# Early sums for the fifth down product, and the running sum's start copied on chip

## The chip, the cores and the metric

The kernel runs on one core of a Trainium2 chip. Its time is the device time in microseconds, the median of several executions. Everything is float32: each matmul operand is split into a high and a low part of type fp32r, and a product is three matmuls (high x high, high x low, low x high).

## The reference, cut to what matters

```python
def conv_ffn(x, norm_g, w_up, conv_w, conv_b, w_down):
    h = rms_norm(x, norm_g)
    a, b = jnp.split(h @ w_up, 2, axis=-1)
    a = causal_depthwise_conv(a, conv_w) + conv_b      # width 3
    return (jax.nn.silu(a) * b) @ w_down

def reference(x, ...):
    for l in range(2):                                 # DEPTH
        x = x + hybrid_mixer(x, ...)                   # attention and retention
        x = x + conv_ffn(x, ...)
    return rms_norm(x, final_norm)
```

The input is 512 tokens by 1024; w_down is 2816 by 1024. The change touches only the last product of each layer, `g @ w_down`.

## The kernel before, in words

**The down projection.** `g` (2816 x 512 tokens) and `w_down` are cut into 2 x 2 quarters and multiplied with 7 quarter products instead of 8 (the scheme of Strassen and Winograd). The weights' quarters are W11, W21, W12 and W22; four products take a single quarter or W12 + W22, and three take a running sum that grows in place from W11: W11 + W12, then + W22, then + W21. Each quarter comes in 6 pieces (`PIECES`), five of 128 x 1024 numbers (524288 bytes) and a last one of half that. So there are 7 x 6 = 42 *units* (`UNITS_DOWN`), and unit u is piece u % 6 of product u // 6:

- k = 0: W11; k = 1: W11 + W12; k = 2: + W22; k = 3: W21; k = 4, the fifth: W12 + W22; k = 5: W22; k = 6: the full running sum.
- The raw weights of k = 0, 3, 4 and 5 are loaded into *raw slots*: 4 in `w_raw` (numbers 0 to 3) and 4 in `far_raw` (4 to 7, `FAR` on). The low part of a unit takes the place of its raw data. For k = 1, 2 and 6 the raw data is in `t_raw`, six tiles for the running sum, and the raw slot holds only the low part.
- The high part of a unit goes into one of 8 *high slots* (`w_hi`, `far_hi`), in turn.
- `RAW_ORDER`, `RAW_SLOT`, `HI_ORDER` and `HI_SLOT` (lines 63 to 68) are these plans, written out by hand.

**Who does what.** Each engine has its own list of work and goes through it in order; a wait holds up all that stands behind it.

- SyncE (`load_down`, line 575) issues the plain loads. The 6 pieces of the running sum's W11 (`load_sum`, line 571) and those of units 1 to 3 alternate while the last up product runs. Then each further unit is loaded when its raw slot is free, that is when TensorE is done with the slot's earlier unit (semaphore `s_unit`), in the order in which slots come free: units 18, 19, 24, 25, 20, 21, 22, 23, 26, 27, 28 and so on. Units 26 and 27 take the slots of units 18 and 19. After them come the first four slabs of the next layer.
- GpSimd issues the accumulating transfers, which add a piece from memory onto a tile: `first_sums` (line 700) adds W12 onto the running sum, `gated` multiplies the last pair of g, `further_sums` (line 706) adds W22 and then W21 onto the running sum, each piece when VectorE has made the low part that used the sum before it (`s_qlo`), and then adds W22 onto the raw data of the fifth product's units 24 to 29, each when W21's sum of the same piece (`s_tsum[j]`) and the unit's load (`s_fetch`) have landed.
- ScalarE makes the high parts (`unit_high`, line 864) and those of `g`'s chunks (`chunk_high`, line 879), four units ahead of TensorE. Among the first units stand `last_quarter`, `tap` and `silu` of the last pair.
- VectorE makes the low parts (`unit_low`, line 1412; `chunk_low`, line 1421) three units ahead, the sums of chunks, and takes the products out of PSUM.
- TensorE (`down_unit` in layer 0, `token_unit` in layer 1) runs a unit as 24 matmuls of 256 columns in layer 0 and 12 of 512 in layer 1, after the waits for `s_qlo` and, at even units, `s_clo` (the chunk's low part). A chunk of g serves two units. All matmuls come out of the helper `three_open`, lines 1768 to 1770.

The lines of the profile that matter below: L569 the load of a unit, L573 that of the running sum, L697 an accumulating transfer onto the running sum, L717 one onto a unit of the fifth product, L727 GpSimd's product of the last pair, L877 a unit's high part, L891 and L893 a chunk's, L854 the last quarter of the up products, L862 and L1400 the convolution, L1418 a unit's low part, L1427 and L1429 a chunk's.

Of the kernel before, what the change touches and what calls it, by code (L numbers as in the profile page):

```python
# [61 lines left out]
FAR = RING  # L62
RAW_ORDER = [3, 1, 0, 2, FAR, FAR + 1, FAR + 2, FAR + 3, 3, 1, FAR + 2, FAR + 3, 3, 1, FAR + 2, FAR + 3, 3, 1,
             0, 2, FAR + 2, FAR + 3, 3, 1, FAR, FAR + 1, 0, 2, FAR + 2, FAR + 3, 3, 1, FAR, FAR + 1, 0, 2,
             FAR, FAR + 1, FAR + 2, FAR + 3]
RAW_SLOT = [RAW_ORDER + [FAR, FAR + 1], RAW_ORDER + [3, 1]]
HI_ORDER = [(2, 1, 0, FAR, FAR + 1, FAR + 2, FAR + 3, 3)[u % 8] for u in range(UNITS_DOWN)]
HI_SLOT = [HI_ORDER[:39] + [FAR, FAR + 1, 3], HI_ORDER]
HI_AFTER = (0, 1, 2, 3, 4, 5, 6, 7)
# [3 lines left out]
def before(slots, u):  # L73

    return max((v for v in range(u) if slots[v] == slots[u]), default=None)

# [78 lines left out]
def trunk(nc, xt, wts, wdn, par, consts, rope, decay, last, out):  # L155
    with ExitStack() as ctx:
# [32 lines left out]
        far_hi = sb("far_hi", [P, 4, SLAB], F32R, u_lo_at)  # L189
        w_hi_at = at[0]  # L190
# [213 lines left out]
        s_tland = [sem(f"s_tland{j}") for j in range(2)]  # L404
# [6 lines left out]
        s_unit = sem("s_unit")  # L411
        s_gain = sem("s_gain")
# [54 lines left out]
        def slot_raw(s):  # L467

            return w_raw[:, s, :] if s < RING else far_raw[:, s - RING, :]

        def slot_lo(s):

            return w_lo[:, s, :] if s < RING else far_lo[:, s - RING, :]
# [44 lines left out]
        def _(sp):  # L518
# [46 lines left out]
            def load_unit(l, u):  # L565
# [3 lines left out]
                sp.dma_start(unit_raw(l, u), wdn[l * 4 + quarter, :, j * 1024:j * 1024 + piece(j)]).then_inc(s_fetch[RAW_SLOT[l][u]], 16)  # L569

            def load_sum(l, j):

                sp.dma_start(t_raw[:, j, 0:piece(j)], wdn[l * 4 + W11, :, j * 1024:j * 1024 + piece(j)]).then_inc(s_tland[int(j > 1)], 16)  # L573

            def load_down(l):
# [3 lines left out]
                for k in range(3):  # L579
                    sp.wait_ge(s_prod, done + k + 1)  # L580
                    load_sum(l, 2 * k)
                    load_sum(l, 2 * k + 1)
# [5 lines left out]
                for u in sorted(LOADED[PIECES:], key=lambda u: before(RAW_SLOT[l], u)):  # L588
                    sp.wait_ge(s_unit, l * UNITS_DOWN + before(RAW_SLOT[l], u) + 1)
                    load_unit(l, u)  # L590
# [61 lines left out]
        def _(pool):  # L652
# [47 lines left out]
            def first_sums(l):  # L700

                for j in range(PIECES):
                    pool.wait_ge(s_tland[int(j > 1)], l * (32 + 32 * (j > 1)) + 32 + 32 * (j > 1))
                    add_piece(l, j, W12)
# [1535 lines left out]
```

## Time and profile before

| | us |
|---|---|
| median of 3 runs | 1579.28 |
| lowest and highest | 1578.63, 1582.32 |
| the profiled execution | 1583.04 |
| its span in the profile | 1581.2 |
| TensorE busy | 1563.6 |
| VectorE busy | 1163.5 |
| ScalarE busy | 768.9 |
| GpSimd busy | 250.8 |

The times of the rows below are counted from the start of the profiled execution's span; what the span leaves out of its time is 1.8 us. The down projection runs from 674 to 789 us in layer 0 and from 1458 to 1575 us in layer 1. In the page's rows a group ends with its idle time and what ended it; in a timeline the bracket says how long the engine stood idle and who released it.

### The profile page before, as it was taken

To read this page: it belongs to the slowest core of one execution; us is meant where nothing else is said; L and a number is where in the kernel's file an instruction comes from. 1 tells how busy PE (TensorE), PEld (TensorE's weight loads), DVE (VectorE), ACT (ScalarE), POOL (GpSimd) and SP (SyncE) were. 2 spreads that over 40 slices of the span, in tenths; PEclk is the share of its full clock that TensorE was granted. 3 is DMA by queue.
4 is the path that set the end of the run, shared out by engine and by line. 5 is a ranking of instruction groups with operands and counts; after the bars stand their busy time and mean duration, and the time that the engine had idled before them with its cause. 6 is when DMAs were issued, how large, how long until landed. Compare 5 with 4: busy or idle time off the path is not lost.

```text
span 1581.2 us, 22764 instructions
## 1 busy us (share of the span) xinstructions
PE 1563.6 (99%) x9106; PEld 1379.8 (87%) x9106; DVE 1163.5 (74%) x1295; ACT 768.9 (49%) x982; POOL 250.8 (16%) x270
## 2 busy tenths in 40 slices
PE   9999999999999999999999999999999999999988
PEld 7888888888888999999988888888888899999866
DVE  7257876786679787796972678667766897777967
ACT  5344334542355555663533533355422565556636
POOL 4000000000230222331240000000002212223400
PEclk9999999999999999999999999999999999999999
DMA  5342222222227888999133422222223388888991
GB/s 195 97 122 78 78 81 93 80 68 93 93 94 239 240 240 241 280 224 275 67 104 97 120 78 76 75 92 80 68 93 101 103 248 235 238 241 275 231 267 53
DMA packets 66628, 231.41 MB, mean 146 GB/s; under 512 B 7392, under 2 KB 7904, under 8 KB 66528
## 3 DMA queue, kind: packets, MB, share of 16 engines
q1 hardware_dynamic: 52272, 182.93, 33.7%
q0 software_dynamic: 12096, 41.95, 14.6%
q10 hardware_dynamic: 2160, 5.12, 1.2%
q8 instruction: 72, 1.18, 0.3%
q14 instruction: 28, 0.23, 0.0%
HBM read 225.78 MB, written 2.10 MB: 144 GB/s over the span
## 4 chain that ended last, share of the span: by engine, by line
PE 91%; DMA 4%; issue 2%; DVE 1%; POOL 1%; ACT 0%; DVEq 0%; POOLq 0%
PE ps L1762 18%; PE ps L1764 18%; PE ps L1763 18%; PE ps L1768 10%; PE ps L1770 10%; PE ps L1769 10%; DMA far_raw<-wdn 2%; PE ps L1891 1%; DMA w_raw<-wdn 1%; PE ps L1880 1%; PE ps L1858 1%; PE ps L1862 1%; DMA w_raw<-wts 1%; DMA far_raw<-wts 1%; POOL g_raw L727 1%
## 5 line engine op out<-in xcount | busy, mean ns | idle before, releaser
L1762 PE MATMUL ps<-u_hi,w_hi 128*128 128x512 f32 x768 | 301.3, 392 | 0.0
L1763 PE MATMUL ps<-u_lo,w_hi 128*128 128x512 f32 x768 | 299.3, 390 | 0.0
L1764 PE MATMUL ps<-u_hi,w_lo 128*128 128x512 f32 x768 | 299.1, 389 | 0.0
L1200 DVE TENSOR_TENSOR w_lo<-w_raw,w_hi 128x1024 fp32r<-128x1024 f32 x158 | 208.5, 1332 | 68.3 <-ACT w_hi L766 68.1
L766 ACT ACTIVATE w_hi<-w_raw 128x1024 fp32r<-128x1024 f32 x158 | 164.1, 1052 | 77.3 <-DMA w_raw<-wts 70.9
L1764 PEld LDWEIGHTS ps<-u_hi,w_lo 128*128 128x128 f32 x768 | 144.2, 188 | 30.4
L1762 PEld LDWEIGHTS ps<-u_hi,w_hi 128*128 128x128 f32 x768 | 144.4, 188 | 28.4
L1763 PEld LDWEIGHTS ps<-u_lo,w_hi 128*128 128x128 f32 x768 | 144.4, 188 | 28.3
L1768 PE MATMUL ps<-comb_hi,far_hi 128*128 128x256 f32 x576 | 161.1, 280 | 0.6 <-DVE far_lo L1363 0.2
L1769 PE MATMUL ps<-comb_lo,far_hi 128*128 128x256 f32 x576 | 160.8, 279 | 0.0
L1770 PE MATMUL ps<-comb_hi,far_lo 128*128 128x256 f32 x512 | 142.9, 279 | 0.0
L1768 PE MATMUL ps<-comb_hi,w_hi 128*128 128x256 f32 x432 | 121.6, 282 | 0.6 <-DVE cb L1385 0.3
L1769 PE MATMUL ps<-comb_lo,w_hi 128*128 128x256 f32 x432 | 120.7, 279 | 0.0
L1770 PE MATMUL ps<-comb_hi,w_lo 128*128 128x256 f32 x432 | 120.6, 279 | 0.0
L1768 PEld LDWEIGHTS ps<-comb_hi,far_hi 128*128 128x128 f32 x576 | 108.1, 188 | 1.5 <-issue 1.1
L1769 PEld LDWEIGHTS ps<-comb_lo,far_hi 128*128 128x128 f32 x576 | 108.1, 188 | 0.0
L727 POOL TENSOR_TENSOR g_raw<-cc,cb 128x512 f32<-128x512 f32 x36 | 73.6, 2063 | 185.5 <-ACT cc L848 185.5
L1770 PEld LDWEIGHTS ps<-comb_hi,far_lo 128*128 128x128 f32 x512 | 96.1, 188 | 0.0
L1363 DVE TENSOR_TENSOR far_lo<-far_raw,far_hi 128x1024 fp32r<-128x1024 f32 x48 | 58.6, 1222 | 42.3 <-ACT far_hi L835 42.3
L1768 PEld LDWEIGHTS ps<-comb_hi,w_hi 128*128 128x128 f32 x432 | 81.0, 188 | 2.3 <-DVE cb L1385 1.3
L1769 PEld LDWEIGHTS ps<-comb_lo,w_hi 128*128 128x128 f32 x432 | 81.1, 188 | 0.0
L1770 PEld LDWEIGHTS ps<-comb_hi,w_lo 128*128 128x128 f32 x432 | 81.1, 188 | 0.0
(307 smaller groups left out, 3715.8 us busy)
## 6 DMA issues: line engine op xcount, KB each, us to landing
w_raw<-wts SPq DMA_DIRECT2D x212, 512.0 KB, 3.5
far_raw<-wts SPq DMA_DIRECT2D x56, 512.0 KB, 4.2
t_raw<-wdn POOLq DMA_DIRECT2D x30, 512.0 KB, 9.8
w_raw<-wdn SPq DMA_DIRECT2D x24, 512.0 KB, 7.6
w_raw<-wts POOLq DMA_DIRECT2D x18, 512.0 KB, 10.5
far_raw<-wts POOLq DMA_DIRECT2D x16, 512.0 KB, 7.2
far_raw<-wdn SPq DMA_DIRECT2D x16, 512.0 KB, 8.7
t_raw<-wdn SPq DMA_DIRECT2D x10, 512.0 KB, 5.7
```

What stands on the lines that cost most here:

```text
L727: nc.gpsimd.tensor_tensor(g_raw[:, f, :], cc[:, h, :], cb[:, h, :], ALU.mult).then_inc(s_gf, 1)
L766: nc.scalar.activation(w_hi[:, s, :], w_raw[:, s, :], ACT.Copy).then_inc(s_hi, 1)
L1200: nc.vector.tensor_tensor(w_lo[:, s, :], w_raw[:, s, :], w_hi[:, s, :].bitcast(F32), ALU.subtract).then_inc(s_lo, 1)
L1363: nc.vector.tensor_tensor(part_lo(l, n, k), part_raw(l, n, k), part_hi(l, k).bitcast(F32), ALU.subtract).then_inc(s_elo, 1)
L1762: nc.tensor.matmul(dst, a_hi, b_hi, start=start, stop=False)
L1763: nc.tensor.matmul(dst, a_hi, b_lo, start=False, stop=False)
L1764: return nc.tensor.matmul(dst, a_lo, b_hi, start=False, stop=stop)
L1768: nc.tensor.matmul(dst, a_hi, b_hi, start=start, stop=False, skip_group_check=True)
L1769: nc.tensor.matmul(dst, a_hi, b_lo, start=False, stop=False, skip_group_check=True)
L1770: return nc.tensor.matmul(dst, a_lo, b_hi, start=False, stop=stop, skip_group_check=True)
L1858: nc.tensor.matmul(psf[:, E0 + BLK[c]:E0 + BLK[c] + WIDTH[c]], q2[:, h, t * P:(t + 1) * P], k2[:, h, 0:WIDTH[c]], start=(c != 3), stop=Fal ...
L1862: mm = nc.tensor.matmul(psf[:, E0 + BLK[c]:E0 + BLK[c] + WIDTH[c]], q_lo[p][:, h % 2, t * P:(t + 1) * P], k2[:, h, 0:WIDTH[c]], start=Fals ...
```

## The change

- Two *spare* raw slots, 8 and 9 (`SPARE`), lie in the place of the high slots 6 and 7. These two serve as high slots once each, for units 5 and 6; from unit 8 on the high parts go round 6 slots instead of 8. Units 26 and 27 are loaded into the spare slots when units 5 and 6 are done (`vacated`), and the slots of the later units move with them. Units 36 to 41 use the two as well, for their low parts.
- The sums W12 + W22 of the fifth product's first four pieces (`EARLY_SUMS`) are issued between the W22 and the W21 sums of the running sum; those of units 28 and 29 stay behind the W21 sums.
- The running sum's W11 is no longer loaded: ScalarE copies each of units 0 to 5 from its raw slot into `t_raw`, just ahead of making its high part. `first_sums` waits for the copy.

```diff
--- before.py
+++ after.py
@@ -60,12 +60,14 @@
 UNITS_DOWN = 7 * PIECES
 CHUNKS = 21
 FAR = RING
+SPARE = FAR + 4
 RAW_ORDER = [3, 1, 0, 2, FAR, FAR + 1, FAR + 2, FAR + 3, 3, 1, FAR + 2, FAR + 3, 3, 1, FAR + 2, FAR + 3, 3, 1,
-             0, 2, FAR + 2, FAR + 3, 3, 1, FAR, FAR + 1, 0, 2, FAR + 2, FAR + 3, 3, 1, FAR, FAR + 1, 0, 2,
-             FAR, FAR + 1, FAR + 2, FAR + 3]
-RAW_SLOT = [RAW_ORDER + [FAR, FAR + 1], RAW_ORDER + [3, 1]]
-HI_ORDER = [(2, 1, 0, FAR, FAR + 1, FAR + 2, FAR + 3, 3)[u % 8] for u in range(UNITS_DOWN)]
+             0, 2, FAR + 2, FAR + 3, 3, 1, FAR, FAR + 1, SPARE, SPARE + 1, 0, 2, FAR + 2, FAR + 3, 3, 1, FAR, FAR + 1,
+             SPARE, SPARE + 1, FAR + 2, FAR + 3, FAR, FAR + 1]
+RAW_SLOT = [RAW_ORDER, RAW_ORDER]
+HI_ORDER = [(2, 1, 0, FAR, FAR + 1, FAR + 2, FAR + 3, 3)[u] if u < 8 else (FAR + 1, 3, 2, 1, 0, FAR)[u % 6] for u in range(UNITS_DOWN)]
 HI_SLOT = [HI_ORDER[:39] + [FAR, FAR + 1, 3], HI_ORDER]
+EARLY_SUMS = 4
 HI_AFTER = (0, 1, 2, 3, 4, 5, 6, 7)
 SUM_K = (1, 2, 4, 5)
 
@@ -73,6 +75,13 @@
 def before(slots, u):
 
     return max((v for v in range(u) if slots[v] == slots[u]), default=None)
+
+
+def vacated(l, u):
+
+    if RAW_SLOT[l][u] >= SPARE and before(RAW_SLOT[l], u) is None:
+        return HI_SLOT[l].index(RAW_SLOT[l][u] - 2)
+    return before(RAW_SLOT[l], u)
 
 
 LOADED = [u for u in range(UNITS_DOWN) if u // PIECES in (0, 3, 4, 5)]
@@ -187,6 +196,9 @@
         u_lo_at = at[0]
         u_lo = sb("u_lo", [P, KT, S], F32R)
         far_hi = sb("far_hi", [P, 4, SLAB], F32R, u_lo_at)
+        spare_at = u_lo_at + 2 * 4 * SLAB
+        spare_raw = sb("spare_raw", [P, 2, SLAB], F32, spare_at)
+        spare_lo = sb("spare_lo", [P, 2, SLAB], F32R, spare_at)
         w_hi_at = at[0]
         w_hi = sb("w_hi", [P, RING, SLAB], F32R)
         w_odd = sb("w_odd", [P, RING, SLAB], F32, w_hi_at)
@@ -401,7 +413,7 @@
         s_c11 = sem("s_c11")
         s_c21 = sem("s_c21")
         s_c22 = sem("s_c22")
-        s_tland = [sem(f"s_tland{j}") for j in range(2)]
+        s_tcopy = sem("s_tcopy")
         s_tsum = [sem(f"s_tsum{j}") for j in range(PIECES)]
         s_qhi = sem("s_qhi")
         s_qlo = sem("s_qlo")
@@ -409,6 +421,7 @@
         s_clo = sem("s_clo")
         s_csum = sem("s_csum")
         s_unit = sem("s_unit")
+        s_spare = sem("s_spare")
         s_gain = sem("s_gain")
         s_tok = sem("s_tok")
         s_moved = sem("s_moved")
@@ -466,11 +479,11 @@
 
         def slot_raw(s):
 
-            return w_raw[:, s, :] if s < RING else far_raw[:, s - RING, :]
+            return w_raw[:, s, :] if s < RING else far_raw[:, s - RING, :] if s < SPARE else spare_raw[:, s - SPARE, :]
 
         def slot_lo(s):
 
-            return w_lo[:, s, :] if s < RING else far_lo[:, s - RING, :]
+            return w_lo[:, s, :] if s < RING else far_lo[:, s - RING, :] if s < SPARE else spare_lo[:, s - SPARE, :]
 
         def slot_hi(s):
 
@@ -566,11 +579,8 @@
 
                 k, j = divmod(u, PIECES)
                 quarter = {0: W11, 3: W21, 4: W12, 5: W22}[k]
-                sp.dma_start(unit_raw(l, u), wdn[l * 4 + quarter, :, j * 1024:j * 1024 + piece(j)]).then_inc(s_fetch[RAW_SLOT[l][u]], 16)
-
-            def load_sum(l, j):
-
-                sp.dma_start(t_raw[:, j, 0:piece(j)], wdn[l * 4 + W11, :, j * 1024:j * 1024 + piece(j)]).then_inc(s_tland[int(j > 1)], 16)
+                landed = s_fetch[RAW_SLOT[l][u]] if RAW_SLOT[l][u] < SPARE else s_spare
+                sp.dma_start(unit_raw(l, u), wdn[l * 4 + quarter, :, j * 1024:j * 1024 + piece(j)]).then_inc(landed, 16)
 
             def load_down(l):
 
@@ -578,15 +588,13 @@
                 load_unit(l, 0)
                 for k in range(3):
                     sp.wait_ge(s_prod, done + k + 1)
-                    load_sum(l, 2 * k)
-                    load_sum(l, 2 * k + 1)
                     load_unit(l, k + 1)
                 sp.wait_ge(s_prod, done + 4)
                 load_unit(l, 4)
                 sp.wait_ge(s_prod, done + 5)
                 load_unit(l, 5)
-                for u in sorted(LOADED[PIECES:], key=lambda u: before(RAW_SLOT[l], u)):
-                    sp.wait_ge(s_unit, l * UNITS_DOWN + before(RAW_SLOT[l], u) + 1)
+                for u in sorted(LOADED[PIECES:], key=lambda u: vacated(l, u)):
+                    sp.wait_ge(s_unit, l * UNITS_DOWN + vacated(l, u) + 1)
                     load_unit(l, u)
                 for i in range(RING if l + 1 < DEPTH else 0):
                     sp.wait_ge(s_unit, l * UNITS_DOWN + max(u for u in range(UNITS_DOWN) if RAW_SLOT[l][u] == i) + 1)
@@ -700,22 +708,35 @@
             def first_sums(l):
 
                 for j in range(PIECES):
-                    pool.wait_ge(s_tland[int(j > 1)], l * (32 + 32 * (j > 1)) + 32 + 32 * (j > 1))
+                    pool.wait_ge(s_tcopy, l * PIECES + j + 1)
                     add_piece(l, j, W12)
 
+            def add_fifth(l, j):
+
+                u = 4 * PIECES + j
+                if RAW_SLOT[l][u] >= SPARE:
+                    pool.wait_ge(s_spare, 32 * (l + 1))
+                else:
+                    pool.wait_ge(s_fetch[RAW_SLOT[l][u]], 16 * (1 + l * arrivals_of_layer(u) + arrivals(u)))
+                nc.gpsimd.dma_start(unit_raw(l, u), wdn[l * 4 + W22, :, j * 1024:j * 1024 + piece(j)],
+                                    accum_op=ALU.add).then_inc(s_tsum[j], 16)
+
             def further_sums(l):
 
-                for k, quarter in ((1, W22), (2, W21)):
-                    for j in range(PIECES):
-                        pool.wait_ge(s_qlo, l * UNITS_DOWN + k * PIECES + j + 1)
-                        add_piece(l, j, quarter)
                 for j in range(PIECES):
-                    u = 4 * PIECES + j
-                    s = RAW_SLOT[l][u]
+                    pool.wait_ge(s_qlo, l * UNITS_DOWN + PIECES + j + 1)
+                    add_piece(l, j, W22)
+                for j in range(EARLY_SUMS):
+                    pool.wait_ge(s_tsum[j], l * 64 + 32)
+                    add_fifth(l, j)
+                for j in range(PIECES):
+                    pool.wait_ge(s_qlo, l * UNITS_DOWN + 2 * PIECES + j + 1)
+                    if j < EARLY_SUMS:
+                        pool.wait_ge(s_tsum[j], l * 64 + 48)
+                    add_piece(l, j, W21)
+                for j in range(EARLY_SUMS, PIECES):
                     pool.wait_ge(s_tsum[j], l * 64 + 48)
-                    pool.wait_ge(s_fetch[s], 16 * (1 + l * arrivals_of_layer(u) + arrivals(u)))
-                    nc.gpsimd.dma_start(unit_raw(l, u), wdn[l * 4 + W22, :, j * 1024:j * 1024 + piece(j)],
-                                        accum_op=ALU.add).then_inc(s_tsum[j], 16)
+                    add_fifth(l, j)
 
             def gated(l, n):
 
@@ -864,16 +885,19 @@
             def unit_high(l, u):
 
                 k, j = divmod(u, PIECES)
-                if k in (1, 2, 6):
-                    act.wait_ge(s_tsum[j], l * 64 + {1: 16, 2: 32, 6: 48}[k])
-                elif k == 4:
-                    act.wait_ge(s_tsum[j], l * 64 + 64)
+                if k in (1, 2):
+                    act.wait_ge(s_tsum[j], l * 64 + 16 * k)
+                elif k in (4, 6):
+                    act.wait_ge(s_tsum[j], l * 64 + (48 if (k == 4) == (j < EARLY_SUMS) else 64))
                 else:
                     act.wait_ge(s_fetch[RAW_SLOT[l][u]], 16 * (1 + l * arrivals_of_layer(u) + arrivals(u)))
                 if before(HI_SLOT[l], u) is None:
                     act.wait_ge(s_prod, 7 * (l * SPLIT + SPLIT - 1) + HI_AFTER[u])
                 else:
                     act.wait_ge(s_unit, l * UNITS_DOWN + before(HI_SLOT[l], u) + 1)
+                if k == 0:
+                    act.wait_ge(s_prod, 7 * (l * SPLIT + SPLIT - 1) + j // 2 + 1)
+                    nc.scalar.activation(t_raw[:, j, 0:piece(j)], unit_raw(l, u), ACT.Copy).then_inc(s_tcopy, 1)
                 nc.scalar.activation(slot_hi(HI_SLOT[l][u])[:, 0:piece(j)], unit_raw(l, u), ACT.Copy).then_inc(s_qhi, 1)
 
             def chunk_high(l, c):
```

## Rows read from the trace of the kernel before

**Rows 1.** The page: busy time, share of the span, instructions, by engine.

```profile
PE 1563.6 (99%) x9106; PEld 1379.8 (87%) x9106; DVE 1163.5 (74%) x1295; ACT 768.9 (49%) x982; POOL 250.8 (16%) x270
```

**Rows 2.** Waits of TensorE, whole run: us in total, times, longest.

```profile
PE ps L1768 <- DVE chunk_lo L1429: 6.5, 6, 1.8
```

**Rows 3.** TensorE's timeline: start us, us, instruction, [idle before <- releaser].

```profile
685.39 0.28 PE L1768 MATMUL ps<-chunk_hi,far_hi 128*128 128x256 f32 x1
...
752.07 0.42 PE L1768 MATMUL ps<-chunk_hi,far_hi 128*128 128x256 f32 x1 [1.78 <-DVE chunk_lo L1429]
...
1470.76 0.48 PE L1768 MATMUL ps<-far_hi,chunk_hi 128*128 128x512 f32 x1
...
1518.85 0.47 PE L1768 MATMUL ps<-far_hi,chunk_hi 128*128 128x512 f32 x1 [0.51 <-DVE chunk_lo L1429]
...
1529.60 0.47 PE L1768 MATMUL ps<-w_hi,chunk_hi 128*128 128x512 f32 x1 [0.96 <-DVE chunk_lo L1429]
...
1534.59 0.50 PE L1768 MATMUL ps<-far_hi,chunk_hi 128*128 128x512 f32 x1 [2.02 <-DVE w_lo L1418]
...
1539.43 0.47 PE L1768 MATMUL ps<-far_hi,chunk_hi 128*128 128x512 f32 x1 [1.82 <-DVE chunk_lo L1429]
...
1541.45 0.63 PE L1769 MATMUL ps<-far_lo,chunk_hi 128*128 128x512 f32 x1
```

**Rows 4.** Stretches: length, busy by engine, PEclk, DMA share, GB/s.

```profile
665.00:670.00 5.00, 5.00 (x44) 5.00 (x43) 3.53 (x5) 5.00 (x7) 5.00 (x4) 1.00 1.03 414
1485.00:1490.00 5.00, 5.00 (x26) 4.15 (x24) 4.79 (x6) 3.79 (x5) 1.71 (x2) 1.00 1.07 211
1540.00:1545.00 5.00, 5.00 (x17) 3.94 (x16) 5.00 (x6) 3.20 (x4) 0.00 (x0) 0.66 0.00 1
```

**Rows 5.** The chain that ended last, layer 1: start us, us, step.

```profile
1510.22 9.57 DMA w_raw<-wdn
...
1522.86 13.21 DMA far_raw<-wdn
1536.09 1.07 ACT far_hi L877
```

**Rows 6.** GpSimd's timeline, layer 0 and layer 1.

```profile
699.13 0.87 POOL L697 DMA_DIRECT2D t_raw<-wdn  x1 [0.60 <-DVE far_lo L1418]
...
1485.34 0.86 POOL L697 DMA_DIRECT2D t_raw<-wdn  x1 [0.61 <-DVE far_lo L1418]
...
1520.32 0.86 POOL L717 DMA_DIRECT2D w_raw<-wdn  x1 [18.04 <-DMA w_raw<-wdn]
```

**Rows 7.** Landing of the sums issued at 1485, 1498, 1500, 1520 (four), 736.

```profile
DMA to landing us min/median/max: 9.8/9.8/9.8
...
DMA to landing us min/median/max: 11.0/11.6/12.2
...
DMA to landing us min/median/max: 15.3/16.7/18.1
...
DMA to landing us min/median/max: 5.7/11.9/15.2
...
DMA to landing us min/median/max: 12.6/13.5/14.5
```

**Rows 8.** ScalarE's timeline, layer 0 and layer 1.

```profile
666.18 1.05 ACT L891 ACTIVATE chunk_hi<-g_raw 128x1024 fp32r<-128x1024 f32 x1
...
674.14 0.60 ACT L854 ACTIVATE ca<-ps 128x512 f32<-128x512 f32 x1
...
1450.69 1.05 ACT L891 ACTIVATE chunk_hi<-g_raw 128x1024 fp32r<-128x1024 f32 x1
...
1461.26 0.58 ACT L854 ACTIVATE ca<-ps 128x512 f32<-128x512 f32 x1
```

**Rows 9.** VectorE's timeline, layer 0.

```profile
677.15 0.74 DVE L1400 SCALAR_TENSOR_TENSOR cc<-ca,pars,cc 128x512 f32<-128x512 f32 x1
...
682.32 2.06 DVE L1427 SCALAR_TENSOR_TENSOR chunk_lo<-g_raw,chunk_hi 128x768 fp32r<-128x768 f32 x1
```

## The prediction

> **What bounds the kernel now.** I read the page first: TensorE is busy 99% of a span of 1581.2 us [rows 1]. So a change that takes nothing away from TensorE can win only where TensorE stands still. The second view, its waits, puts almost all of that on one line, the matmul of the split products, which waits for VectorE's low parts [rows 2]. The third, TensorE's timeline, says where. I call the pieces of the down projection's weights units, 0 to 41, in the order of use (unit = 6 x product + piece), and count products from 0; the fifth product is k = 4, units 24 to 29. A full unit takes 2.72 us in layer 1 (12 matmuls, 0.227 us apart). In layer 1 the restarts at 1518.85, 1529.60, 1534.59 and 1539.43 are the first matmuls of units 22, 26, 27 and 28 [rows 3]: three of the four are of the fifth product. The matmuls between them are left out there, a full unit being 12 of them. From start to start the intervals before them are 0.7, 1.1, 2.3 and 2.1 us above 2.72, and units 22, 28 and 29 themselves take 0.1, 1.4 and 0.3 too long; in sum **8.0 us**. The 1.4 is the clock: from 1541 us on matmuls start 0.43 us apart, and the stretch 1540 to 1545 shows a granted clock of 0.66 after the three idle spells [rows 3, 4]: some of its time at 1.2 GHz instead of 2.4. In layer 0 the same four restarts (at 733.21, 744.06, 747.22 and 752.07; the last stands in [rows 3], and all are in the sum of [rows 2]) give 0.8, 1.0, 0.4 and 2.1, and 1.6 goes to the clock: **5.9 us**. All that this change can win is so 13.9 us, 0.9%.
>
> Why they are late: the chain of waits goes from TensorE at 1510 to the reload of a raw slot (9.6 us), to GpSimd's accumulating transfer for unit 28 (13.2 us), to ScalarE's high part, to VectorE's low parts, to the matmul at 1539.43 [rows 3, 5]. GpSimd's timeline shows the hole: after the sums of units 24 and 25, issued at 1500, it waits 18.0 us, until 1520.32, for unit 26's raw data [rows 6], whose slot comes free only with unit 18. But the last views say that the transfers were hardly idle meanwhile: a stretch with sums alone moves 211 GB/s, one with mostly plain loads 414 [rows 4], so a sum of 524288 bytes takes 2.5 us of the engines and a load 1.27. The sums issued at 1498.2 and 1499.6 land after 11.0 and 12.2 us, those of units 24 and 25 after 15.3 and 18.1 [rows 7]: at 1509.2, 1511.8, 1515.5 and 1518.8. That is 3.84 us for each full sum where loads run beside them (9.6 us for 2.5 sums, piece 5 being half a piece).
>
> **The change part by part.**
>
> 1. *The running sum's W11 from the chip.* Removed: 6 loads a layer on SP's queue (5.5 full ones, 7 us of transfer time), just ahead of the units' loads. On the rule: the Trainium skill, page "DMA: Bandwidth & Descriptors", section on bandwidth, puts loads from HBM at about 358 GB/s; by it the loads cost 8.1 us instead of 7; the row shows 414 and decides, and the sum below would stay. Added: 6 copies on ScalarE ahead of units 0 to 5's high parts. Two such operations back to back start 0.95 us apart, so 5.3 us a layer. Behind them on ScalarE are the last quarter, the taps and SiLU of the last pair. From the chunk copy at 666.18 there are now 12 operations to the last quarter, 11.4 us: it starts at about 677.6 in layer 0 instead of 674.14 [rows 8], and VectorE's convolutions, which started at 677.15, start when the first tap is done, at 679.1 [rows 9]. VectorE runs without a gap there (the chunk's low part, 2.06 us from 682.32, ended at 684.4) [rows 9], and TensorE takes that chunk at 685.39 [rows 3]. It is now ready at 686.4: **a new stall of 1.1 us at unit 4 of layer 0**. In layer 1 ScalarE had stood waiting for landings, which now come earlier: counted from the same chunk copy, 1450.69 + 11.4 is 1462.1, 0.8 us behind the 1461.26 of before [rows 8]; the stall is 0.3 (unit 4 starts at 1470.76 [rows 3], with 0.7 us to spare, and VectorE comes 1.0 later). The first W22 sum is issued 2 us (layer 0) and 1 us (layer 1) later. The copies' waits for s_prod cost nothing: ScalarE has waited for the fourth part product before (chunk 0).
>
> 2. *Units 26 and 27 in the spare tiles.* Their loads move from after units 18 and 19 to after units 5 and 6, at about 1476 and 1479 on SP's queue, ahead of those of units 20 on. That adds 2.5 us of transfers where the W22 sums run; the W11 loads had left some 3 us of backlog there, which goes. The high parts' ring shrinks from 8 to 6. ScalarE makes them at most some 4 units ahead, so the shorter ring adds no wait.
>
> 3. *The order of the sums.* Before: 6 W22, 6 W21, units 24, 25 | hole | 26, 27, 28, 29. After: 6 W22, units 24 to 27, 6 W21, units 28, 29. Units 26 and 27 are so in time by over 15 us: their stalls go, 2.3 + 1.1 in layer 1 and 1.4 in layer 0. Each of W21's first four waits for the early sum of the same piece, with three more sums in the queue behind it, so the queue doesn't run dry. But **unit 28's sum now stands behind everything**, and waits until W21's fourth piece (counted from 0) has landed.
>
> *When it lands, layer 1.* W22's last sum landed at 1485.34 + 9.8 = 1495.1 [rows 6, 7]; now 0.5 later (1 us of start, 2.5 of loads, less 3 of backlog). Four sums at 2.5 us, as unit 20's load is issued at 1500.7 only: 1505.6. Five W21 sums at 3.84: 1524.8. Then unit 28's own, behind half a sum. Nearest rows: of the four sums issued from 1520.32 on, the first, with nothing ahead, took 5.7 us [rows 7], the third, unit 28's, with two ahead, 13.2 [rows 5], and by the median of 11.9 between second and third the second, with one ahead, 10.6 [rows 7]. I take 8.1, the middle of 5.7 and 10.6: 1532.9. From landing to matmul it took 1539.43 - 1536.1 = 3.3 us, so TensorE starts unit 28 at 1536.2 instead of 1539.43: **3.2 us gained**. Without the stalls of units 26 to 28 TensorE would be there at 1534.2 (1539.43 - 1.1 - 2.3 - 2.1, and the 0.3), so 2.0 us of waiting are left. Bounds: 5.7 us at the least gains 2 us more, which ends the wait; 13.2 us costs 5.1, a loss of 1.9.
>
> *Layer 0.* W22's last sum, issued at 699.13, also took 9.8 us and landed at 708.9 [rows 6]; now 2.1 + 2.5 - 3 = 1.6 later, 710.5. Unit 20's load goes out at 714.1, so only three sums run at 2.5 us: 718.0. Six at 3.84: 741.0. Plus 8.1 and 3.3: 752.4, against 752.07 [rows 3] (before, the sum was issued at 736.2 and landed after 12.6 us, at 748.8 [rows 7]). **Nothing gained (-0.3)**; the stall at unit 4 is swallowed, since the sums, not TensorE, set that time.
>
> 4. *What stays.* Unit 22's stall (0.7 and 0.8 us) is a plain load that goes out when TensorE leaves unit 16 and takes as long as the 9.6 us one of the chain [rows 5]; its slot and the company it has stay. The clock fell after idle spells of which the last, 1.8 us in both layers, are like what is left; I let it fall again. The next layer's first slabs are loaded earlier; TensorE doesn't wait for them before either.
>
> Sum: -3.2 + 0.3 = 2.9 us less. The profiled execution took 1583.0 us (span 1581.2, 1.8 around it), 3.8 above the median of the three runs, whose spread is 3.7; I take the 2.9 from the median 1579.28 and get **1576.5 us**.
>
> **The rivals.** *No stall at unit 28.* If the sums keep 2.5 us beside the loads, nine sums after 1495.6 end at 1518, unit 28's lands by 1526 and TensorE never waits: 8.0 - 0.8 = 7.2 us in layer 1, 5.9 - 0.8 = 5.1 in layer 0, less 1.4 of new stalls: 10.9 us, 1568.4. For it: the rate of sums alone. Against: the four landings from 1509 to 1519. 0.17.
> *The stall stays and the clock doesn't fall*, being one spell and not three: 1.5 us more in each layer, 1573.5. Against: layer 0 fell after only 0.8, 0.3 and 1.8 us. 0.13.
> *Slower*: unit 28 is the price. It decides once its sum lands after 1536.1 (748.8 in layer 0), which is so if the sum takes over 11.3 us beside the loads of units 30 to 33, as the one of 13.2 did. At 13.2 both layers lose 5.1 more: 1576.5 + 10.2 = 1586.7 at the worst, half of it 1581.6; past 1584 it is slower. 0.13.
> *Nothing moves*: the sums end when they did, since their number is the same and only their order differs, 1579 +/- 1. For it: layer 0 above. 0.12.
>
> **How the numbers follow.** My forecast, stalls moved to unit 28 and 3 us won, gets 0.45. About 0.3%, 4.7 us, is what a measurement of this kernel can tell from no change: 1574.5 and 1584.0 are the bounds. Faster: the first two rivals, 0.17 + 0.13 = 0.30. Same: 0.45 + 0.12 = 0.57. Slower: 0.13. The range reaches down to the case with no stall, 1568, and up past the middle of the slower case to 1585.
>
> **What would show it.** Right: no idle time before units 26 and 27 in either layer; one wait of 1 to 3 us at unit 28 that ends with the accumulating transfer into w_raw (its slot is now 0); W21 sums issued from about 1498 on with gaps of 2.5 us, not at the low parts' pace; GpSimd's 18.0 us wait gone and one of some 15 us before unit 28's sum; 12 copies into t_raw on ScalarE and no t_raw loads on SP's queue; a new wait of about 1 us at unit 4 of layer 0; a clock under 0.8 after unit 28. Wrong: no wait at unit 28, or one of over 5 us; idle TensorE in units 6 to 21 (a high part held back by the ring of 6, or W22's sums late by the two loads).

## The result, and the profile after

The changed kernel takes 1587.27 us, the median of 8 executions (1583.36 to 1588.42). The kernel before, run beside it, takes 1579.38 (8 executions, 1574.94 to 1582.32). The ratio is 1.0041, with a 95% interval from 1.0030 to 1.0053: **slower by 6.5 us** by the ratio (7.9 by the two medians), more than the 4.7 us that the prediction takes as what can be told from no change. It is the case that the prediction calls "slower", and lies above the range.

| | before [rows 1] | after |
|---|---|---|
| profiled execution | 1583.04 | 1587.19 |
| TensorE idle for VectorE's chunk parts | 6.5 us, 6 times, longest 1.8 [rows 2] | 13.7 us, 7 times, longest 5.1 |
| ScalarE busy, instructions | 768.9, 982 | 779.3, 994 |

The page of the kernel after: busy time by engine.

```profile
PE 1562.8 (99%) x9106; PEld 1379.5 (87%) x9106; DVE 1163.5 (73%) x1295; ACT 779.3 (49%) x994; POOL 250.7 (16%) x270
```

TensorE's waits, whole run (us in total, times, longest); it answers to [rows 2].

```profile
PE ps L1792 <- DVE chunk_lo L1453: 13.7, 7, 5.1
```

TensorE's timeline of the kernel after (start us, us, instruction, idle before it and releaser); it answers to [rows 3].

```profile
692.32 0.36 PE L1792 MATMUL ps<-chunk_hi,far_hi 128*128 128x256 f32 x1 [0.76 <-DVE chunk_lo L1453]
...
735.59 0.36 PE L1792 MATMUL ps<-chunk_hi,w_hi 128*128 128x256 f32 x1 [1.75 <-DVE chunk_lo L1453]
...
756.96 0.55 PE L1792 MATMUL ps<-chunk_hi,w_hi 128*128 128x256 f32 x1 [5.13 <-DVE chunk_lo L1453]
...
1523.56 0.47 PE L1792 MATMUL ps<-w_hi,chunk_hi 128*128 128x512 f32 x1 [1.11 <-DVE chunk_lo L1453]
...
1528.46 0.47 PE L1792 MATMUL ps<-far_hi,chunk_hi 128*128 128x512 f32 x1 [0.54 <-DVE chunk_lo L1453]
...
1543.57 0.47 PE L1792 MATMUL ps<-w_hi,chunk_hi 128*128 128x512 f32 x1 [3.97 <-DVE chunk_lo L1453]
```

These are the first matmuls of units 6, 22 and 28 in layer 0, and of units 22, 24 and 28 in layer 1 (unit 24 of layer 0 waited 0.47 us and is not shown). No restart stands at units 26 and 27 any more, in either layer. One stands at unit 28, of 5.1 and 4.0 us; none of those of before was over 2.02 [rows 3].

GpSimd's timeline of the kernel after, layer 1; it answers to [rows 6].

```profile
1490.78 2.09 POOL L721 DMA_DIRECT2D far_raw<-wdn  x2
1497.46 1.74 POOL L721 DMA_DIRECT2D spare_raw<-wdn  x2 [4.58 <-DMA spare_raw<-wdn]
1504.67 0.86 POOL L705 DMA_DIRECT2D t_raw<-wdn  x1 [5.47 <-DMA far_raw<-wdn]
1513.76 2.63 POOL L705 DMA_DIRECT2D t_raw<-wdn  x3 [2.95 <-DMA spare_raw<-wdn]
1531.35 0.86 POOL L721 DMA_DIRECT2D w_raw<-wdn  x1 [14.96 <-DMA t_raw<-wdn]
```

The sums of units 24 to 27 are out by 1499 and the hole of 18.0 us is gone. In its place GpSimd waits 15.0 us, until W21's piece 4 has landed, before it may issue unit 28's sum.

The landing of the sums in the kernel after, from issue: the last W22 sum (1490.25), the three W21 sums of 1514, unit 28's sum (1531.35); then the plain loads issued from 1510 to 1518. It answers to [rows 7].

```profile
DMA to landing us min/median/max: 11.4/11.4/11.4
...
DMA to landing us min/median/max: 13.9/16.8/18.8
...
DMA to landing us min/median/max: 8.9/8.9/8.9
...
DMA to landing us min/median/max: 10.0/12.5/13.4
```

The chain that ended last, layer 1 (start us, us, step); it answers to [rows 5].

```profile
1514.32 13.19 DMA w_raw<-wdn
1527.55 3.79 issue
1531.35 8.87 DMA w_raw<-wdn
1540.24 1.06 ACT w_hi L901
1541.33 1.22 DVE w_lo L1442
1542.56 0.88 DVE chunk_lo L1453
1543.57 0.47 PE ps L1792
```

The first step is unit 28's plain load. The 3.79 us called "issue" is no work of GpSimd: its timeline above puts that wait down to the transfer into t_raw, W21's piece 4, issued at 1514.3 and landed 16.8 us later, at 1531.1. The sum itself then takes 8.87 us, and 3.3 us lie from its landing to the matmul, as before.

### The profile page after: what moved, and what is told of

It is laid out like the page before. It is cut to its first block, busy times and chain, and to the rows that moved or that the text cites. A ratio compares the mean times of both kernels' runs of the same rounds, so it can differ in the third digit from the quotient of the medians.

```text
span 1585.4 us, 22772 instructions
## 1 busy us (share of the span) xinstructions
PE 1562.8 (99%) x9106; PEld 1379.5 (87%) x9106; DVE 1163.5 (73%) x1295; ACT 779.3 (49%) x994; POOL 250.7 (16%) x270
## 4 chain that ended last, share of the span: by engine, by line
PE 51%; DMA 3%; DVE 2%; issue 1%; ACT 1%; DVEq 0%; POOLq 0%
PE ps L1786 9%; PE ps L1788 9%; PE ps L1787 9%; PE ps L1792 7%; PE ps L1794 7%; PE ps L1793 7%; DMA w_raw<-wdn 3%; PE ps L1915 1%; PE ps L1904 1%; DMA w_raw<-wts 0%; PE ps L1882 0%; PE ps L1886 0%; DVE far_lo L1442 0%; PE ps L2039 0%; PE ps L1926 0%
## 5 line engine op out<-in xcount | busy, mean ns | idle before, releaser
L1793 PEld LDWEIGHTS ps<-comb_lo,w_hi 128*128 128x128 f32 x432 | 81.1, 188 | 0.0
## 6 DMA issues: line engine op xcount, KB each, us to landing
t_raw<-wdn POOLq DMA_DIRECT2D x30, 512.0 KB, 11.6
w_raw<-wts POOLq DMA_DIRECT2D x18, 512.0 KB, 10.1
```

The source lines that it names most:

```text
L1793: nc.tensor.matmul(dst, a_hi, b_lo, start=False, stop=False, skip_group_check=True)
```

## The experiments

A measure that serves all of them, worked out from the starts of units in TensorE's timeline: the time from the start of unit 0 to that of unit 28, and to that of unit 36, in each layer. It leaves out what the rest of the kernel adds. Each row is one profiled execution. In layer 0 the matmuls of 256 columns run at one of several paces, which no edit chose (see the last section). In "another order alone", at 113.3 ns a matmul, unit 28 comes after 72.1 us, 1.1 of them waiting; in "six early sums, W11 loaded", at 120.0 ns, after 74.9 with no wait. So a difference of up to 4 us in layer 0 between rows with short waits or none need be no effect of an edit.

| kernel | median us | to unit 28, layer 0 / 1 | to unit 36, both layers |
|---|---|---|---|
| before, the profile of the rows | 1579.38 | 78.1 / 81.0 | 201.1 |
| before, profiled again | | 78.2 / 78.2 | 195.8 |
| after | 1587.27 | 81.2 / 81.0 | 203.5 |
| after, profiled again | 1586.01 | 80.9 / 81.1 | 204.6 |
| early sums, W11 loaded | 1585.24 | 79.5 / 81.6 | 204.2 |
| copies alone | 1581.83 | 80.9 / 80.3 | 200.1 |
| no early sums | 1579.86 | 79.4 / 78.2 | 196.2 |
| six early sums | 1568.27 | 74.1 / 74.7 | 187.4 |
| six early sums, W11 loaded | 1567.63 | 74.9 / 74.7 | 188.8 |
| another order alone | 1571.06 | 72.1 / 76.2 | 187.7 |
| six early sums, the last pair's product earlier | 1570.58 | 74.1 / 74.7 | 187.4 |

**1. The early sums alone.** The changed kernel, but W11 is loaded onto the running sum as before.

```diff
+                    load_sum(l, 2 * k)
+                    load_sum(l, 2 * k + 1)
                     load_unit(l, k + 1)
...
-                    pool.wait_ge(s_tcopy, l * PIECES + j + 1)
+                    pool.wait_ge(s_tland[int(j > 1)], l * (32 + 32 * (j > 1)) + 32 + 32 * (j > 1))
...
-                    nc.scalar.activation(t_raw[:, j, 0:piece(j)], unit_raw(l, u), ACT.Copy).then_inc(s_tcopy, 1)
```

> The changed kernel with the running sum's W11 loaded from memory again, as before the change; the early sums and the spare slots stay. Theory A (the queue of sums sets unit 28): the copies only delayed the start of the W22 sums by 1.9 us in layer 0 and 0.8 us in layer 1, so unit 28's wait shrinks by about that, the 0.9 us stall at unit 6 of layer 0 goes, and the rest of the wait, 3 us or more in each layer, stays: 1 to 3 us faster than the changed kernel, still slower than or the same as before. Theory B (the on-chip copies are what costs): the loss of 6.5 us goes altogether, the time is that of before or better and unit 28's wait is under 1.5 us.

Measured: 1585.24 (12 executions), ratio 1.0034 [1.0021, 1.0047]. TensorE's waits, its first matmul of unit 28 in layer 0, and GpSimd's issue of unit 28's sum in layer 1:

```profile
PE ps L1795 <- DVE chunk_lo L1456: 10.6, 6, 3.4
...
755.16 0.55 PE L1795 MATMUL ps<-chunk_hi,w_hi 128*128 128x256 f32 x1 [3.44 <-DVE chunk_lo L1456]
...
1530.31 0.86 POOL L727 DMA_DIRECT2D w_raw<-wdn  x1 [14.96 <-DMA w_raw<-wdn]
```

The loss is there without the copies: by the ratios 5.4 of the 6.5 us come with the order and the tiles. The wait at unit 28 is 3.4 us in layer 0 and 3.1 in layer 1, as forecast, the one at unit 6 is gone, and GpSimd's wait of 15.0 us stands unchanged. In layer 1 unit 4 waited 1.1 us here, which was not forecast.

**2. The copies alone.** The kernel before, with W11 copied by ScalarE and not loaded; slots and order as before.

```diff
-                    load_sum(l, 2 * k)
-                    load_sum(l, 2 * k + 1)
...
+                if k == 0:
+                    act.wait_ge(s_prod, 7 * (l * SPLIT + SPLIT - 1) + j // 2 + 1)
+                    nc.scalar.activation(t_raw[:, j, 0:piece(j)], unit_raw(l, u), ACT.Copy).then_inc(s_tcopy, 1)
```

> The kernel before with only the W11 copies on ScalarE; ring, slots and order of sums of before. Theory A: stall of 1 us at unit 4 to 6 of layer 0, W22 sums start 2 us later there; units 26 to 28 wait as before (their stalls hang on the reload of unit 26's slot): within 2 us of before. Theory B: slower than before by 4 us or more.

Measured: 1581.83 (11 executions), ratio 1.0015 [1.0005, 1.0025], 2.4 us slower, a little more than the 2 us expected. TensorE's waits, the first matmul of unit 26 in layer 0, the stretch behind it (length, busy by engine, PEclk, DMA share, GB/s), and the landing of the last W22 sum in layer 1:

```profile
PE ps L1765 <- DVE chunk_lo L1426: 9.6, 6, 5.4
...
749.18 0.55 PE L1765 MATMUL ps<-chunk_hi,w_hi 128*128 128x256 f32 x1 [5.40 <-DVE chunk_lo L1426]
...
745.00:750.00 5.00, 0.82 (x4) 0.85 (x5) 2.36 (x2) 2.64 (x3) 0.00 (x0) 0.58 1.06 274
...
DMA to landing us min/median/max: 8.1/8.1/8.1
```

Without the W11 loads the last W22 sum lands after 8.1 us instead of 9.8 [rows 7]: the backlog that they left is worth 1.7 us, not 3. In layer 0 the wait at unit 26 grew from 0.8 us to 5.4, and the trace divides the 4.6 us. Counted from unit 0, unit 26's sum is issued 1.4 us later (61.1 against 59.7) and takes 8.8 us instead of 6.8, so it lands 3.4 us later; and TensorE comes 1.2 us earlier, at 113.3 ns a matmul instead of 118.7.

**3. All six sums early.** The changed kernel with one number changed.

```diff
-EARLY_SUMS = 4
+EARLY_SUMS = 6
```

> The changed kernel with EARLY_SUMS = 6: all six sums of the fifth product ahead of the W21 sums. Theory A: unit 28's sum no longer waits for W21's piece 4 but for its own load, which has the transfer engines more to itself, and lands at least 4 us earlier in each layer; unit 28 waits under 1 us, the clock stays at full speed, unit 22's stall shrinks; the W21 sums land by about 1550, ahead of unit 36: 10 us faster than the changed kernel, some 4 faster than before. Theory B: no faster than the changed kernel. A rival to A: the total work of the transfer engines is the bound, so the W21 sums are late for units 36 on and the wait reappears there, with the time of the changed kernel.

Measured: 1568.27 (5 executions), ratio 0.9922 [0.9905, 0.9939]: **some 12 us faster than before** (12.3 by the ratio, 11.1 by the medians), where some 4 were expected. TensorE's only wait of this kind (us in total, times, longest) and the matmul behind it, unit 6 of layer 0; GpSimd's timeline in layer 1, with the sums of units 28 and 29 and then five of W21's; and the landing of the loads issued from 1501 to 1509:

```profile
PE ps L1792 <- DVE chunk_lo L1453: 0.7, 1, 0.7
...
692.29 0.36 PE L1792 MATMUL ps<-chunk_hi,far_hi 128*128 128x256 f32 x1 [0.69 <-DVE chunk_lo L1453]
...
1509.68 0.86 POOL L721 DMA_DIRECT2D w_raw<-wdn  x1 [19.86 <-DMA w_raw<-wdn]
1511.50 0.86 POOL L721 DMA_DIRECT2D w_raw<-wdn  x1 [0.96 <-DMA w_raw<-wdn]
1512.04 4.74 POOL L705 DMA_DIRECT2D t_raw<-wdn  x5
...
DMA to landing us min/median/max: 2.8/4.1/5.3
```

GpSimd waits longer here than before, 19.9 us against 18.0 [rows 6], and it costs nothing, because what stands behind is not needed soon: W21's sums serve unit 36. All stalls of the fifth product are gone, unit 22's too. The loads land in 2.8 to 5.3 us, as no sums compete with them meanwhile.

**4. No early sum.** `EARLY_SUMS = 0` in the changed kernel: copies, spare tiles and the ring of 6 stay, the order is that of before.

> The changed kernel with EARLY_SUMS = 0: slots and early loads of units 26 and 27 and the copies stay, but the order of the sums is that of before, W21 ahead of the fifth product. Theory A: the queue has no hole and no sum waits for another's landing except unit 28's for its load (landed at 1527.5 in the changed kernel), so unit 28's sum lands 3 to 4 us earlier than in the changed kernel: its wait falls to 1 us or less, 6 to 9 us faster than the changed kernel. If instead unit 28's place behind all other sums is what costs (it stands behind the same number here), the wait stays at 4 to 5 us.

Measured: 1579.86 (12 executions), ratio 1.0004 [0.9992, 1.0016]. TensorE's first matmul of unit 26 in layer 0, then GpSimd's issue of unit 28's sum and TensorE's first matmul of unit 28 in layer 1:

```profile
747.63 0.36 PE L1792 MATMUL ps<-chunk_hi,w_hi 128*128 128x256 f32 x1 [1.17 <-DVE chunk_lo L1453]
...
1523.22 0.86 POOL L721 DMA_DIRECT2D w_raw<-wdn  x1 [12.47 <-DMA w_raw<-wdn]
...
1537.20 0.47 PE L1792 MATMUL ps<-w_hi,chunk_hi 128*128 128x512 f32 x1 [1.62 <-DVE chunk_lo L1453]
```

So tiles, ring and copies together cost nothing that shows, and bring nothing: unit 27 no longer waits, but unit 28 still does, 1.6 us in layer 1 and 1.5 in layer 0, and so does unit 26 (0.5 and 1.2). The expectation that unit 28's wait would fall to 1 us or less did not hold; the 7.4 us below the changed kernel's 1587.27 did. Against this run the changed kernel differs only in the order of the sums: its loss is the position of the four early sums and W21's, and with it unit 28's.

**5 and 6. Both kernels once more**, unedited, on another chip, to see how much of the first two profiles is theirs alone.

> The changed kernel once more, nothing edited. It asks how much of its 6.5 us is not in the down stage: in the profiles the down stages (start of unit 0 to start of unit 36, both layers) are 2.4 us longer than before, while the 256-column matmuls of layer 0's up stage start 118.7 ns apart in the changed kernel and 116.7 ns or less in the kernel before. If that pace is a matter of the single execution, it differs between two profiles of one kernel and the medians of many runs carry little of it; if it belongs to the kernel, this profile shows 118.7 ns again in layer 0 from 520 to 670 us, and the time is again 5 to 8 us above before.

> The kernel before once more, nothing edited. If the pace of the 256-column matmuls belongs to the execution, this profile shows another pattern than the first (113.3, 116.7 and 118.7 ns in other places) and unit 0 of layer 0 starts at another time than 673.9; if it belongs to the kernel, the pattern and the 673.9 come back. The stalls at units 22 and 26 to 28 should be there in either case, 5 to 8 us a layer with the slower clock behind them.

Measured: the changed kernel 1586.01 (10 executions), ratio 1.0034 [1.0020, 1.0048]; the profiled execution of the kernel before 1579.94, at its median of 1580.01. Counted from unit 0 of layer 1, the sums of the changed kernel land as in its first profile, unit 28's after 77.7 us in both. The stretches behind unit 28 (length, busy by engine, PEclk, DMA share, GB/s) of the kernel after, first profile:

```profile
755.00:760.00 5.00, 3.04 (x15) 3.07 (x16) 5.00 (x6) 3.41 (x5) 0.00 (x0) 0.66 0.04 9
1545.00:1550.00 5.00, 5.00 (x16) 3.92 (x16) 5.00 (x6) 3.07 (x4) 0.00 (x0) 0.67 0.00 0
```

And TensorE's waits and the same stretches in the second profile of the kernel before:

```profile
PE ps L1768 <- DVE chunk_lo L1429: 6.5, 6, 1.7
PE ps L1768 <- DVE w_lo L1418: 0.5, 1, 0.5
...
750.00:755.00 5.00, 3.25 (x28) 3.08 (x27) 4.32 (x5) 3.37 (x4) 0.00 (x0) 1.00 0.82 275
1540.00:1545.00 5.00, 5.00 (x22) 3.89 (x22) 5.00 (x5) 3.34 (x4) 0.00 (x0) 1.00 0.00 0
```

The clock stays at 1.00, where the profile of the rows had 0.66 [rows 4], and the wait of 2.02 us at unit 27 [rows 3] is one of 0.5. That first execution took 3.8 us more than the median, and these two things are in it: the kernel before has executions with them and without. How many have the fall, the mean granted clock of a whole execution suggests: it was 0.997 in the first profile and 0.999 in the second, and of 55 other executions of the kernel before, 17 had 0.998 or less. All 18 of the changed kernel had 0.995 to 0.998, and it has the fall in both profiles and both layers. Its second profile had 0.50 in the stretch 755 to 760.

**7. Six early sums, W11 loaded.** Edits 1 and 3 together.

> All six sums of the fifth product ahead of W21's, and W11 loaded from memory instead of copied: does the copy help once the order is right? Theory A: the 7 us of loads stand in the transfer queue ahead of the W22 sums, where there is slack once unit 28's sum is early; the 0.9 us stall at unit 6 of layer 0 goes: the time of the run with six early sums and copies (0.992 of before), within 2 us. If the copies matter, 3 us or more slower than that run.

Measured: 1567.63 (6 executions), ratio 0.9925 [0.9911, 0.9938], as with the copies (0.9922): they neither help nor cost once the order is right. The stall at unit 6 of layer 0 is gone with them, as in experiment 1.

**8. Another order alone.** The kernel before, with its slots, its ring and its loads; only the W21 sums are issued behind those of the fifth product.

```diff
-                for k, quarter in ((1, W22), (2, W21)):
-                    for j in range(PIECES):
-                        pool.wait_ge(s_qlo, l * UNITS_DOWN + k * PIECES + j + 1)
-                        add_piece(l, j, quarter)
+                for j in range(PIECES):
+                    pool.wait_ge(s_qlo, l * UNITS_DOWN + PIECES + j + 1)
+                    add_piece(l, j, W22)
...
+                for j in range(PIECES):
+                    pool.wait_ge(s_qlo, l * UNITS_DOWN + 2 * PIECES + j + 1)
+                    pool.wait_ge(s_tsum[j], l * 64 + 48)
+                    add_piece(l, j, W21)
```

> The kernel before with one edit: W21's sums are issued behind the fifth product's instead of ahead; slots, ring of 8 and loads of before. Theory A (what stands in the queue ahead of the fifth product's sums is what matters): GpSimd still waits for unit 26's load, freed by unit 18 at 1510, but the transfer engines are empty by then, so the load takes 4 us instead of 9.6, the sum lands by 1521 and unit 28's by 1529: all stalls from unit 22 on go, and the time is that of the run with six early sums, 9 to 12 us under before. Rival (the spare tiles are needed): units 26 to 28 still wait 2 us or more each layer, the gain is under 5 us.

Measured: 1571.06 (6 executions), ratio 0.9945 [0.9929, 0.9961]. GpSimd's timeline in layer 1 (sums of units 26 to 29, then four of W21's) and the landing of the loads issued from 1500 to 1509:

```profile
1508.60 0.86 POOL L716 DMA_DIRECT2D w_raw<-wdn  x1 [26.59 <-DMA w_raw<-wdn]
1511.28 0.86 POOL L716 DMA_DIRECT2D w_raw<-wdn  x1 [1.81 <-DMA w_raw<-wdn]
1517.41 0.86 POOL L716 DMA_DIRECT2D far_raw<-wdn  x1 [5.28 <-DMA far_raw<-wdn]
1520.52 0.86 POOL L716 DMA_DIRECT2D far_raw<-wdn  x1 [2.25 <-DMA far_raw<-wdn]
1521.06 3.86 POOL L697 DMA_DIRECT2D t_raw<-wdn  x4
...
DMA to landing us min/median/max: 3.5/3.6/3.8
```

An edit of the order brings some 9 of the 12 us with none of the change's parts. Unit 26's slot comes free as late as before, but its load takes some 3.6 us instead of 9.6 [rows 5], and nothing stands ahead of its sum. Not all stalls go, as had been expected: unit 28 still waits 1.1 us in layer 0 and 1.3 in layer 1, for a sum whose load goes out 57.2 us after unit 0; with the change's slots and the same order (experiment 3) it goes out after 51.8, and unit 28 does not wait.

**9. The last pair's product ahead of the last W12 sum.** The stall at unit 6 of layer 0 follows GpSimd's product of the last pair, so with six early sums it was issued one sum earlier.

```diff
-                first_sums(l)
+                first_sums(l, range(PIECES - 1))
                 gated(l, SPLIT - 1)
+                first_sums(l, (PIECES - 1,))
```

> All six early, with copies, and one more edit on GpSimd: the product of the last pair (L748) is issued ahead of the last W12 sum instead of behind it. In the changed kernel that last sum waits for ScalarE's sixth copy, and the product, which slows VectorE's operations beside it from 1.2 to 2.1 us, starts 1.8 us after it otherwise could. If that order makes the 0.9 us stall at unit 6 of layer 0, the stall shrinks to 0.3 us or less and the time is 0 to 1 us under the run with six early sums, which its timing can hardly tell; if the stall comes from ScalarE's copies alone, it stays at 0.9 us.

Measured: 1570.58 (6 executions), ratio 0.9933 [0.9916, 0.9951]: no gain. GpSimd's product, TensorE at unit 6, and ScalarE's SiLU:

```profile
683.40 4.23 POOL L748 TENSOR_TENSOR g_raw<-cc,cb 128x512 f32<-128x512 f32 x2 [4.26 <-ACT cc L870]
...
691.82 0.35 PE L1793 MATMUL ps<-chunk_hi,far_hi 128*128 128x256 f32 x1 [0.87 <-DVE chunk_lo L1454]
...
682.70 1.30 ACT L870 ACTIVATE cc<-cc 128x512 f32<-128x512 f32 x2
```

The product starts 0.5 us earlier than in experiment 3 (683.89), and what it waits for is ScalarE. The stall stays at 0.9 us, so GpSimd's queue is not its cause. ScalarE's copies are: without them (experiments 1 and 7) it is gone.

## Why the prediction was wrong, point by point

**Right.** The order's mechanism was told as it is. Units 26 and 27 are in time. "Unit 28's sum now stands behind everything" and waits for W21's piece 4, GpSimd for 15.0 us ("some 15"). The sum then takes 8.9 us (8.1 forecast) and 3.3 to the matmul (3.3). The ring of 6 adds no wait, the clock falls behind unit 28, and the W22 sums start 0.8 us later in layer 1 (1 forecast). The copies' stall came, about 1 us in layer 0, but at unit 6 and not at unit 4: 0.76 of idle time and a slow pair of matmuls. With unit 0's 1.8 us taken off, the last quarter started at 677.6 and the convolutions at 679.1, as forecast; but the chunk for unit 4 was ready at 685.2 and not at 686.4. The low part ahead of it took 1.22 us, where before it had taken 2.35 beside GpSimd's product, which now started later.

**Signs that went the other way.** It named a wait of over 5 us as a sign of being wrong, and layer 0 has one of 5.1. W21's sums were to go out from 1498 on, 39.6 us after unit 0; they went out from 42.1 on, after GpSimd had waited 4.6 us for the loads into the spare tiles and 5.5 for unit 24's sum. (The sum at the end, 1579.28 - 2.9, is 1576.4, not 1576.5.)

**The failing step is the forecast of when unit 28's sum lands.** Counted from unit 0 of the same layer (1458.45 before and 1462.55 after in layer 1; 673.94 and 675.73 in layer 0):

| layer 1, us from unit 0 | forecast | measured |
|---|---|---|
| last W22 sum landed | 37.2 | 39.1 |
| the four early sums landed | 47.2 | 50.7 |
| W21's piece 4 landed | 66.4 | 68.5 |
| unit 28's sum landed | 74.5 | 77.7 |
| unit 28 | 77.8 | 81.0 |

- The last W22 sum is 1.9 us later than forecast in layer 1 (38.8 against 36.6, so 2.2, in layer 0). The step gave the two early loads 2.5 us and took off 3 for the W11 loads. By the time of that one sum from issue to landing the two are not additive. With the copies the early loads add 3.3 us (8.1 in experiment 2, 11.4 after). And beside the early loads the missing W11 loads take off next to nothing (11.5 us in experiment 1, 11.4 after). **The credit of 3 us was worth 0.1** (in layer 0 as well, 11.8 and 11.7).
- Four early sums took 11.6 us instead of 10.0: the rate of 2.5 us is that of sums alone, and the last two of these, 2.8 and 3.8 us apart, had the loads of units 20 and 21 beside them.
- W21's five sums took 3.57 us each instead of 3.84, which gave 1.4 us back; unit 28's own took 1.1 more with its place in the queue. In sum 1.9 + 1.6 - 1.4 + 1.1 = 3.2 us in layer 1. In layer 0 unit 28's sum landed at 77.9 against 75.2, so 2.7 us later, and unit 28 started 2.7 later too (81.2 against 78.5).

**The base was a second failing step.** The 2.9 us were reckoned against one profiled execution that had lost time in ways that most executions do not, and then taken from the median. Against the second profile, which lies at the median, unit 28 came at 78.2 in both layers: the forecast's own 78.5 and 77.8 are then no gain at all. And the fall of the clock, which it kept in both layers, is a cost that the second profile does not have, and by their mean clocks most other executions do not either. Between that profile and the one after, the stage grew by 203.5 - 195.8 = 7.7 us, of which 3.0 and 2.8 are unit 28's delay; the rest, 1.9, lies behind it, where the clock is low. That is the loss of 6.5 to 7.9 us, within what single executions scatter. Over the stage the forecast was 201.1 - 2.9 = 198.2 us: it is 5.3 under the measured 203.5, nearly all of it the late sum (3.2 + 2.7), and its base of 201.1 is 5.3 above the 195.8 of the execution at the median. Each of the two steps so makes about half of the 10.8 us between 1576.5 and 1587.27.

**What was left at "stays".** Unit 22's stall was to stay at 0.7 and 0.8 us. It grew to 1.75 us of idle time in layer 0 and 1.11 in layer 1, and one of 0.5 came up at unit 24. "The company it has" did not stay: the loads of 1510 to 1518 took 10.0 to 13.4 us, against 9.57 of the one in [rows 5]. W21's sums now run there. Unit 22's own load took 10.0 us in layer 1 and 11.1 in layer 0, against 9.4 and 10.1 before. Where no sums ran they took 2.8 to 5.3 us (experiment 3) and 3.5 to 3.8 (experiment 8). The Trainium skill, page "DMA: Bandwidth & Descriptors", section on queues, rings and completion order, says that a DMA engine with work in several queue rows takes a packet of one and then of the next in turn; by that a load shares the engines with every sum under way and is not ahead of them, and the trace agrees.

**The rivals.** "Slower" was the right mechanism with its threshold well placed: unit 28's sum was to decide once it landed after 748.8 in layer 0, and it landed at 753.6, which is 751.8 when the 1.8 us by which unit 0 came later are taken off. In layer 1 it landed at 1540.2, less 4.1 the threshold of 1536.1 itself: against that first profile unit 28 lost nothing there (81.0 us after unit 0 in both), against the second 2.8. Its price was read as a longer sum (13.2 us); it was an issue that came later, with a sum of 8.9. "The stall stays and the clock doesn't fall" is out: it fell in both layers of both profiles. "No stall" needed 2.5 us a sum beside loads; 3.57 were measured. "Nothing moves" held that the number of the sums counts and not their order; the order alone moves the time by 8.7 us (experiment 8). That unit 28 waits so long because of the W21 sums ahead of it is shown by experiment 3, and experiment 4 shows that it is not the tiles, the ring or the copies. How much of it is the semaphore's wait for W21's piece 4, and how much the transfers of W21's sums that run meanwhile, was not tried apart.

## What to carry to other kernels

In a queue of transfers like this one the order should be that of need: the sums issued ahead of their time (W21's, for unit 36) made both the sum and the plain loads behind them late, and moving them back gained 8.7 us with one edit, where spare tiles and copies without it gained nothing. When a change pulls some items of a queue forward, follow the first that stays behind; here that was unit 28, and pulling it forward too turned a loss of 6.5 us into a gain of some 12. And profile the base twice before taking a stall from it as the thing to be won, if its profiled execution does not lie at the median.

## What the runs showed of the hardware

**The matmuls' pace.** A difference of 1 to 2 us in where the stage starts (673.94 and 675.42 in two profiles of the kernel before, 675.73 and 674.62 in two of the one after) comes with no edit. The same stretch of up products in the two profiles of the kernel before (length, TensorE's busy time and matmuls, PEclk, DMA share, GB/s), first the profile of the rows:

```profile
520.00:545.00 25.00, 25.00 (x223) 1.00 0.86 244
```

then the second:

```profile
520.00:545.00 25.00, 25.00 (x213) 1.00 0.86 248
```

At the same granted clock of 1.00 one does 223 matmuls of 256 columns in 25 us, the other 213: 112 and 117 ns each. From the start times there are four such paces, 113.3, 116.7, 118.7 and 120.0 ns apart, each held for 8 to some 150 us; at the changes looked at a gap of 130 ns or more stood between two matmuls. They are in the down stage of layer 0 too: its units ran at 118.7 and then 116.7 ns in the first profile of the kernel before, at 116.7 and 113.3 in the first of the one after, and at 120.0 throughout in experiment 7. The matmuls of 512 columns kept 227 ns in every profile where nothing held them up and the clock was at 1.00. What chooses among the paces is open.

**The clock.** It fell to 0.50, which is 1.2 GHz of 2.4, during or just after each single wait of 3.1 to 5.4 us (experiments 1 and 2, and both layers after). In the kernel before it fell after spells of which the longest was 2.02 us in layer 1 and 1.78 in layer 0 [rows 3] in one execution, and stayed at 1.00 in another with spells up to 1.7 us.

**VectorE beside GpSimd.** While GpSimd's product of the last pair ran (4.23 us from 683.91), two of VectorE's operations took long in the kernel after:

```profile
684.89 2.08 DVE L1451 SCALAR_TENSOR_TENSOR chunk_lo<-g_raw,chunk_hi 128x768 fp32r<-128x768 f32 x1
686.90 1.79 DVE L1442 TENSOR_TENSOR far_lo<-far_raw,far_hi 128x512 fp32r<-128x512 f32 x1
```

The same operations alone take less than half of that: a chunk's low part of 768 columns 0.95 us elsewhere in this trace, and the low part of 512 columns 0.68 in experiment 7, where the product had ended before it. The Trainium skill, page "Advanced Engine Details and Errata", section on GpSimd, says that GpSimd shares a read and a write interface with VectorE, which conflicts among others with VectorE's instructions that have two inputs in on-chip memory; both of these have, and the trace agrees. The operation of 2.06 us in [rows 9], from 682.32, ran partly beside that product too (there 4.13 us from 679.43).
